# Starting the input projection after one eighth of the contraction, with its first sums parked in SBUF

## What is computed

```python
mod = jax.nn.silu(c) @ w_ada + b_ada                       # 2048 -> 6 * 2048, for 1 + 8 conditions
shift1, scale1, gate1, shift2, scale2, gate2 = [t[:, None, :] for t in jnp.split(mod, 6, axis=-1)]
h = rmsnorm(x, norm1_g) * (1 + scale1) + shift1
qa, ka, va, qb, kb, vb, r, log_a = project(h, w_in, ...)   # h @ w_in, 2048 -> 6160
oa = mix_a(qa, ka, va)                                     # dilated attention, biased by rel_bias
ob = mix_b(qb, kb, vb, log_a)                              # gated linear attention
x = x + gate1 * merge_out(oa, ob, r, a_out_g, gla_out_g, w_out, x.dtype)
h2 = rmsnorm(x, norm2_g) * (1 + scale2) + shift2
y, new_hist = conv_ffn(h2, conv_hist, w_up, conv_w, conv_b, w_down)
x = x + gate2 * y
```

## Time and profile before

| | us |
|---|---|
| median of 3 runs | 1544.39 |
| lowest, highest | 1542.82, 1545.78 |
| span of the profiled execution | 1544.0 |
| TensorE busy | 1514.8 (98%) |
| VectorE busy | 875.7 (57%) |
| ScalarE busy | 633.9 (41%) |
| first product of w_in starts | 44.23 |
| chunk 8 of w_in starts | 79.75 |

### The profile page before, as it was taken

One profiled execution on the slowest core, in us unless ns is written; L12 is line 12 of the kernel. 1 busy time (PEld: TensorE's weight loads), 2 busy tenths in 40 slices (PEclk: granted clock), 3 DMA queues, 4 the chain that ended last, 5 costly groups with the idle time before them and its releaser, 6 DMA issues.

```text
span 1544.0 us, 27862 instructions
## 1 busy us (share of the span) xinstructions
PE 1514.8 (98%) x11762; PEld 1372.8 (89%) x11762; DVE 875.7 (57%) x1509; ACT 633.9 (41%) x873; POOL 52.4 (3%) x89
## 2 busy tenths in 40 slices
PE   8999999999999889999999999999999999999999
PEld 4877888888888557768899999999999999999999
DVE  3655676666667435557454555555554565656574
ACT  3433444434445215235333333334333445545453
POOL 2000000001111000000000000000000000000000
PEclk8999999999999999999999999999999999999999
DMA  9998777777777997997644444454545444454541
GB/s 354 400 355 346 307 257 257 257 259 267 255 288 270 413 414 309 422 363 292 251 164 164 164 164 169 159 184 147 188 146 182 163 172 178 166 181 172 178 176 53
DMA packets 62283, 370.98 MB, mean 240 GB/s; under 512 B 7431, under 2 KB 7913, under 8 KB 27081
## 3 DMA queue, kind: packets, MB, share of 16 engines
q1 hardware_dynamic: 56096, 351.08, 60.6%
q0 software_dynamic: 5904, 17.93, 3.4%
q10 hardware_dynamic: 162, 0.22, 0.0%
HBM read 359.32 MB, written 9.88 MB: 239 GB/s over the span
## 4 chain that ended last, share of the span: by engine, by line
PE 89%; DMA 5%; DVE 3%; SPq 2%; ACT 1%; issue 1%; POOL 0%; ACTq 0%; DVEq 0%
PE ps L989 26%; PE ps L990 25%; PE ps L991 25%; PE ps L941 4%; PE ps L934 1%; SPq L710 1%; DMA ring<-in_w_ada_early 1%; DMA ring<-in_w_out 1%; DMA ring<-in_cache_k_win 1%; DMA proj<-in_tables 1%; ACT whi L1501 1%; DVE wlo L2028 1%; PE ps L1321 1%; DMA ring<-in_w_ada 1%; PE ps L1290 1%
## 5 line engine op out<-in xcount | busy, mean ns | idle before, releaser
L989 PE MATMUL ps<-hhi,whi 128*128 128x288 f32 x3136 | 934.0, 298 | 3.1 <-DVE wlo L1871 1.6
L990 PE MATMUL ps<-hlo,whi 128*128 128x288 f32 x3136 | 922.6, 294 | 0.0
L991 PE MATMUL ps<-hhi,wlo 128*128 128x288 f32 x3136 | 922.5, 294 | 0.0
L989 PEld LDWEIGHTS ps<-hhi,whi 128*128 128x128 f32 x3136 | 589.0, 188 | 38.8 <-issue 29.9
L990 PEld LDWEIGHTS ps<-hlo,whi 128*128 128x128 f32 x3136 | 589.2, 188 | 0.7
L991 PEld LDWEIGHTS ps<-hhi,wlo 128*128 128x128 f32 x3136 | 588.9, 188 | 0.0
L1492 ACT ACTIVATE whi<-ring 128x1024 fp32r<-128x1024 f32 x178 | 185.7, 1060 | 200.7 <-PE ps L991 200.7
L1864 DVE TENSOR_TENSOR wlo<-ring,whi 128x1024 fp32r<-128x1024 f32 x178 | 212.0, 1221 | 78.8 <-ACT whi L1492 78.4
L2028 DVE TENSOR_TENSOR wlo<-ring,whi 128x1024 fp32r<-128x1024 f32 x96 | 117.0, 1223 | 79.6 <-ACT whi L1501 79.5
L1501 ACT ACTIVATE whi<-ring 128x1024 fp32r<-128x1024 f32 x96 | 100.8, 1053 | 130.1 <-PE ps L991 114.2
L2545 DVE TENSOR_TENSOR wlo<-ring,whi 128x1024 fp32r<-128x1024 f32 (+1 forms) x94 | 105.7, 1132 | 56.2 <-ACT whi L1805 56.2
(11 more groups left out here) (298 smaller groups left out, 905.4 us busy)
## 6 DMA issues: line engine op xcount, KB each, us to landing
ring<-in_w_up SPq DMA_DIRECT2D x88, 1024.0 KB, 4.8
ring<-in_w_down SPq DMA_DIRECT2D x32, 1408.0 KB, 6.1
ring<-in_w_ada SPq DMA_DIRECT2D x42, 1024.0 KB, 6.8
ring<-in_w_in SPq DMA_DIRECT2D x28, 1024.0 KB, 6.5
ring<-in_w_ada_early SPq DMA_DIRECT2D x22, 1024.0 KB, 7.5
proj<-in_w_ada SPq DMA_DIRECT2D x22, 1024.0 KB, 11.0
ring<-in_w_in_early SPq DMA_DIRECT2D x20, 1024.0 KB, 9.3
ring<-in_w_out SPq DMA_DIRECT2D x16, 1024.0 KB, 13.2
```

Source lines behind the costliest of these rows:

```text
L989: mm(out, w_hi, x_hi, start=start, stop=False)
L990: mm(out, w_hi, x_lo, start=False, stop=False)
L991: return mm(out, w_lo, x_hi, start=False, stop=stop)
```

## The change

The eight slabs of group 0 are laid out anew: slabs 0 to 3 (half a) hold shift and scale of k-tiles 0 and 1, slabs 4 to 7 (half b) those of k-tiles 2 and 3. The first eight chunks become half chunks (`half_chunk`): each holds two k-tiles for four output tiles (a pair of units) in the banks 0, 1, 2 and 4, in the order of `HALVES`: four over k-tiles 0 and 1, four over k-tiles 2 and 3; the fourth and the fifth are of the same tiles and add up in PSUM. The sums of the first three and of the fifth are copied to `proj` (`half_copy`), those of the last three are added onto them. They have weights laid out for them, `w_in_first`. Slabs 4 to 7, the bias products and the second turn come between the half chunks; slab 0 goes ahead of the second half of x's transposes, slab 1 and the roots between them. Modulation is in two parts (`half_mod`, `half_norm`). The eight slabs of group 1 are used two behind each of chunks 4 to 7 and no longer two behind chunks 1, 3, 5 and 7. On ScalarE and VectorE the copies of emptied tiles stand ahead of the splitting of the next weights. On SP the first four w_in loads are asked for between the first w_ada slabs, and lead slabs earlier; some of the later w_ada slabs have new homes (`LEAD_HOMES`), and the counts for the ring's odd slots are shifted to suit. The bias tables are loaded to another place, once x is transposed.

```diff
--- before.py
+++ after.py
@@ -30,6 +30,9 @@
 NC9 = 1 + NB
+PAIR_TILES = (28, 32, 36, 24)
+HALVES = ((0, 0), (0, 1), (0, 2), (0, 3), (1, 3), (1, 0), (1, 1), (1, 2))
+LEAD_HOMES = "SSLLRRSSLLSSRRLLSSLLSSLL"
 DIL = ((128, 1), (512, 4), (2048, 16))
@@ -130,11 +133,17 @@
+    early = np.arange(2 * D).reshape(2, KD // 4, 2, 256)
+    early[:, 0] = early[:, 0].transpose(1, 0, 2).copy()
+    first = column_blocks(w_in[0, 0:D, 2048:5120], 4, 512)[:, 0].reshape(6, P, 4, 512)
+    first = np.stack([first[PAIR_TILES[q] // 4 - 4][:, 2 * z:2 * z + 2] for z, q in HALVES])
+    first = first.reshape(4, 2, P, 1024).transpose(0, 2, 1, 3).reshape(4, P, 2048)
     down = w_down[0].reshape(4, 11, P, D // 256, 256).transpose(3, 0, 2, 1, 4)
...
             "w_down": np.ascontiguousarray(down.reshape(D // 256, 4, P, 11 * 256)),
-            "w_ada_early": column_blocks(w_ada[0, :, 0:2 * D], 4, 512)}
+            "w_in_first": np.ascontiguousarray(first),
+            "w_ada_early": column_blocks(w_ada[0][:, early.reshape(-1)], 4, 512)}
...
@@ -490,6 +504,12 @@
+        def half_banks(r):
+            return (0, 1, 2, 4)[r]
+        def half_tile(j, r):
+            return PAIR_TILES[HALVES[j][1]] + r
         def bank_of(n, t):
@@ -524,27 +544,40 @@
-        ADA_AT = [s // 2 * 2 + 1 for s in range(22)] + [22, 22]
+        ADA_AT = [4 + s // 2 for s in range(8)] + [s // 2 * 2 + 1 for s in range(8, 22)] + [22, 22]
         LATE_AT = [23 + r // 2 * 4 for r in range(32)]
...
+            if s < 4:
+                return 0, (0, 2, 1, 3)[s], 16
             if s < 8:
-                return s // 4, (0, 2, 1, 3, 0, 1, 2, 3)[s], 16
-            a = s - 8
-            return (0, 1 + 2 * (a % 2), 32 + 16 * (a // 4)) if a % 4 < 2 else (2, a % 2, 16 + 16 * (a // 4))
+                return 1, (1, 3, 0, 2)[s - 4], 16
+            a, kind = s - 8, LEAD_HOMES[s - 8]
+            before = LEAD_HOMES[0:a].count(kind) // 2
+            if kind == "S":
+                return 0, 1 + 2 * (a % 2), 32 + 16 * before
+            if kind == "R":
+                return 1, (1, 3)[a % 2], 32 + 16 * before
+            return 2, a % 2, 16 + 16 * before
+        def lead_freed(a):
+            kind = LEAD_HOMES[a]
+            before = [b for b in range(a) if LEAD_HOMES[b] == kind and b % 2 == a % 2]
+            return 8 + before[-1] + 1 if before else a + 1
...
@@ -655,7 +690,7 @@
-                sp.wait_ge(raw_used, a + 5)
+                sp.wait_ge(raw_used, lead_freed(a))
                 ada_load(8 + a)
@@ -671,17 +706,26 @@
                 sp.dma_start(xr[0:NS, 2, cols], a["x_sample"].rearrange("b t d -> (b t) d")[:, cols]).then_inc(x_in[n], 16)
-            for s in range(8):
+            for s in range(3):
                 ada_load(s)
             in_load(0)
+            for s in range(3, 6):
+                ada_load(s)
             in_load(1)
-            for s in range(2):
-                sp.wait_ge(raw_used, s + 3)
-                ada_load(s + 8)
+            for s in range(6, 8):
+                ada_load(s)
+            sp.wait_ge(raw_used, 3)
+            ada_load(8)
+            in_load(2)
+            sp.wait_ge(raw_used, 4)
+            ada_load(9)
+            in_load(3)
             ada_load(10)
...
             ada_load(11)
+            lead_load(4)
+            lead_load(5)
             def unit_used(x):
@@ -713,8 +757,9 @@
-            asks = [(2 * w - 5.3, in_load, w) for w in range(2, 48)]
-            asks += [(ADA_AT[a_ - 4] + 1.2, lead_load, a_) for a_ in range(4, 24)]
+            asks = [(2 * w - 5.3, in_load, w) for w in range(4, 48)]
+            asks += [(ADA_AT[a_ - 6] + 0.5, lead_load, a_) for a_ in (6, 7)]
+            asks += [(ADA_AT[a_ - 4] + 1.2, lead_load, a_) for a_ in range(8, 24)]
             asks += [(LATE_AT[r - 2] + 1.4 if r >= 2 else ADA_AT[20 + r] + 1.2, late_load, r) for r in range(32)]
@@ -800,7 +845,8 @@
-            pool.wait_ge(full[1], 16)
+            pool.wait_ge(*PT_.upto("x15"))
+            pool.wait_ge(*NA[0].upto("q5"))
             c1 = CONST_LAYOUT["hot_s"][0]
...
@@ -951,6 +998,8 @@
                 i, half = s // 8, s // 4 % 2
+                if s == 8:
+                    pe.wait_ge(*PV_.upto("bias_s"))
                 if i and s % 4 == 0:
@@ -961,6 +1010,8 @@
                     pe.wait_ge(*AV.upto("mod", i - 1))
+                elif i == 0:
+                    pe.wait_ge(*PV_.upto("bias_p"))
                 ada_turn(6 if half else 5).then_inc(*AT.step("turn_b" if half else "turn_a"))
@@ -969,20 +1020,19 @@
             vectors()
+            early_slab(0)
             for k in range(8, KD):
                 x_turns(k)
-            for s in range(4):
-                early_slab(s)
-            norm_roots()
+                if k == 11:
+                    early_slab(1)
+                if k == 13:
+                    norm_roots()
+            early_slab(2)
+            idle_products(6, 2)
+            early_slab(3)
+            idle_products(6, 1)
+            early_turn(0, 0)
             idle_products(6, 4)
-            early_slab(4)
-            biases()
-            early_turn(0, 0)
-            for s in range(5, 8):
-                early_slab(s)
-            idle_products(3, 1)
-            early_turn(0, 1)
-            idle_products(7, 8)
@@ -1046,6 +1096,34 @@
                     between(c)
+            def half_chunk(j):
+                z = HALVES[j][0]
+                pe.wait_ge(lo_done, CH_IN + j + 1)
+                for r in range(4):
+                    if j in (1, 2, 3):
+                        pe.wait_ge(part_v if r % 2 else part_a, 2 * (j - 1) + r // 2 + 1)
+                    elif j > 4:
+                        pe.wait_ge(tile_v if r % 2 else tile_a, 2 * (j - 5) + r // 2 + 1)
+                    for k in range(2):
+                        if j in (0, 4):
+                            pe.wait_ge(*NL[0].upto(f"l{2 * z + k}", 0))
+                        w = slice(512 * k + P * r, 512 * k + P * r + P)
+                        last = three(ps[:, half_banks(r), 0:TOK], whi[:, j % BUFS, w], wlo[:, j % BUFS, w],
+                                     hhi[:, 2 * z + k, :], hlo[:, 2 * z + k, :], k == 0 and j != 4, k == 1 and j != 3)
+                    if r < 3:
+                        last.then_inc(tile_done, 1)
+                last.then_inc(used, 1)
+                if j == 0:
+                    early_slab(4)
+                if j == 1:
+                    early_slab(5)
+                    early_slab(6)
+                    biases()
+                    early_slab(7)
+                if j == 2:
+                    early_turn(0, 1)
@@ -1248,10 +1326,12 @@
-            pe.wait_ge(*PV_.upto("bias_s"))
-            pe.wait_ge(*NM[0].upto("ms"))
+            pe.wait_ge(*PV_.upto("x15"))
+            pe.wait_ge(*NM[0].upto("rs"))
             for j in range(LAST):
-                if j < CH_OUT:
+                if j < HALVED:
+                    half_chunk(j)
+                elif j < CH_OUT:
                     in_chunk(j)
...
@@ -1521,16 +1606,37 @@
             root(0, roots)
+            in_hi(0)
             ada_rows(0, 0)
+            norm_hi(0, (0, 1))
+            in_hi(1)
+            def half_copy(j, r):
+                act.wait_ge(tile_done, 3 * j + r + 1)
+                if j >= 2:
+                    act.wait_ge(*PV_.upto("bias_s"))
+                f(proj[:, half_tile(j, r), :], ps[:, half_banks(r), 0:TOK], ACT.Copy).then_inc(tile_a if j == 4 else part_a, 1)
+            half_copy(0, 0)
+            half_copy(0, 2)
+            in_hi(2)
+            in_hi(3)
+            half_copy(1, 0)
+            half_copy(1, 2)
             ada_rows(0, 1)
-            in_hi(0)
-            norm_hi(0)
-            for j in range(1, 4):
-                in_hi(j)
+            half_copy(2, 0)
+            in_hi(4)
+            half_copy(2, 2)
+            norm_hi(0, (2, 3))
+            in_hi(5)
+            half_copy(4, 0)
+            half_copy(4, 2)
+            in_hi(6)
+            in_hi(7)
...
                 act.wait_ge(used, CH_IN + BUFS + j + 1)
-                act.wait_ge(*PV_.upto("bias_s"))
+                act.wait_ge(tile_a, j)
                 f(proj[:, UNITS[CHUNKS[j][0]], :], ps[:, early_banks(j)[0], 0:TOK], ACT.Copy).then_inc(tile_a, 1)
@@ -1640,8 +1746,8 @@
-            for j in range(1, LAST):
-                if j <= FIRST:
+            for j in range(HALVED - 3, LAST):
+                if HALVED < j <= FIRST:
                     early_copy(j - 1)
...
@@ -1897,17 +2003,23 @@
-            def norm_roots():
+            def norm_sums():
...
                 v.tensor_scalar(roots, roots, 1 / D, EPS, ALU.mult, ALU.add).then_inc(*NM[0].step("ms"))
+            def norm_diagonals():
                 dve.wait_ge(*NA[0].upto("rs"))
...
                 last.then_inc(*NM[0].step("diag"))
+            def norm_roots():
                 dve.wait_ge(*NT[0].upto("roots"))
@@ -2020,9 +2132,42 @@
+            def half_mod(z):
```

(86 more changed lines are left out.)

49 lines of the change are left out of this document (31 added, 18 removed).

## The result

The changed kernel takes 1546.62 us in the median (1543.74 to 1549.6, 20 runs), the kernel before 1543.97 (1542.52 to 1545.78, 20 runs). The ratio is 1.0018, 95% interval 1.0012 to 1.0024: slower by 0.18%, just within the 0.2% that the prediction called no change. Predicted were 1540.0 and a range of 1537.7 to 1545.0, so the time lies above the range.

A forecast was written before the change was run, and what follows sets the result against it. TensorE alone was taken to set the pace from 44.2 us, so only the opening could win: first product 11.1 us earlier, less added work, 4.4 gained off the 1544.39 median, 1540.0 us; range 1537.7 to 1545.0.

The forecast's parts named there:

- I take the early side: Opening, TensorE's clock: full clock back by 24 us, since slabs come sooner; first product 32.6 to 33.9, taken as 33.1.
- The late end of the bounds: Opening: no clock rise before slab 3 has ended, first product at 38.7, gain -1.1 us.
- That copies go ahead of the next weights' parts costs nothing, as the weights' parts are three chunks ahead: ScalarE and VectorE queues during the half chunks: emptied tiles copied before the next weights are split, at zero cost.
- The prediction's list of landings: DMA arrivals of slabs and loads after the opening, at 2.55 us each; smallest margin at slabs 16, 17.
- The early clock: Opening at full clock by 24 us, all margins holding: 1540.0 us, chance 0.55, own range 1538.5 to 1541.3.
- no idle ahead of chunk 4 over 1 us: Sign that the forecast is right: TensorE waits no more than 1 us before chunk 4.
- What that start has to carry: TensorE from first product to chunk 8: 42.2 us with added slabs, biases and turn; chunk 8 at 75.3, 4.4 gained.
- at 2.55 us each: DMA transfers after the opening: 2.55 us for each MB, giving landings with uses 2 to 7 us later.
- The transfers become the bound: Rival, DMA: at 2.8 us per MB instead of 2.55 the gain shrinks to 0, 1544 us; chance 0.10.
- ScalarE waiting for w_in slabs: Sign of transfers as the bound, alongside TensorE waiting for slabs 5 to 7 or 14 to 17.
- the 27th slab: DMA: with slower transfers this slab would be 6.5 us late against a margin of 1.5 to 2.
- The shift travels to the end unchanged: After the opening: later stages are released by what products have used, so the opening's shift should reach the end.

The follow-up runs named there:

- slab_pair: Changed kernel with slab 1 directly behind slab 0, ahead of the second half of x's transposes; 1546.20 us, ratio 1.0020.
- warm: Changed kernel with four more idle products, two ahead of the condition's turns and two ahead of the small vectors; 1548.36 us, ratio 1.0031.
- kept_low8_less: kept_low8 without the three idle products on either side of slab 3; 1542.57 us, ratio 0.9987.
- after_third: Changed kernel, unedited, profiled a third time; 1544.35 us (one run).
- low8_behind: Changed kernel with VectorE's low part of chunk 8 moved behind chunk 5's adds; 1543.46 us, ratio 0.9998.
- kept_low8: Changed kernel with the edits of kept_clock and low8_behind together; 1541.54 us, ratio 0.9986.
- kept_clock: Changed kernel with nine idle products among x's first eight transposes and ahead of the small vectors, fourth w_ada slab asked before first w_in; 1546.45 us, ratio 1.0012.
- before_kept: Kernel before with nine idle products, behind each of x's first eight k-tiles and ahead of the small vectors; 1546.05 us, ratio 1.0017.
- again: Changed kernel once more, no edit, second profile; 1547.68 us, ratio 1.0021.

## Why the prediction was wrong

**"I take the early side" was the first step that failed.** The term is the clock's. With the rise by 24 us it gave a first product at 32.6 to 33.9; the three profiles have 38.49, 38.61 and 35.66, with the clock back at 33.8, 33.1 and 25.6. The late end of the bounds, 38.7, was right for two of three. The reason given, that slabs had raised the clock before and now come sooner, fell in slab_pair. The Trainium skill's page "TensorE: Matmul & The Clock Gate" (Part 4, PE-mode transpose) says that transposes don't engage the full clock, and read strictly it spoke for the late end; the traces side with it as far as x's second half goes, and warm adds that TensorE fell to 1.2 GHz while it did nothing but transposes. But eighteen transposes from 10.14 us ran at 2.4 GHz behind the idle products, and the changed kernel stayed at 1.2 GHz through slabs too, so the page alone would not have given 33.8 or 25.6.

**"That copies go ahead of the next weights' parts costs nothing, as the weights' parts are three chunks ahead" was the second, and it decides the sign.** I asked what a chunk loses if its own weights' part is late, and did not ask what stands behind that part in VectorE's queue. Being three chunks ahead is what hurts: the part of chunk 8 comes between chunk 4's copies and chunk 5's adds, and needs a load that lands at 65.1 to 67.0 us however early the opening is (69.1 in warm; asked for at 56.3 in kept_low8_less, landing at 66.0, and at 60.5 in after_third, landing at 67.0). The prediction's list of landings leaves this load out; between lead slab 5 (63) and 6 (68), by its 2.55 us each, there is room for it at some 65.5, an estimate; the profiles have 65.1 to 67.0. The early clock that I forecast would have met it: the first product at 33.1 puts chunk 6 at 63.6, and the landing at 66.7 plus 2.83 at 69.5, a wait of 5.9 us. That the order is the cause is shown by moving one line: low8_behind against the changed kernel (3.2 us of the median, each taken beside the kernel before: ratios 0.9998 and 1.0018), and kept_low8 against kept_clock in one session (4.9). No run moved the load instead, ahead of the w_ada slabs that are asked for before it; whether that would do as well is open. My check was "no idle ahead of chunk 4 over 1 us"; it held, and was two chunks too early.

**"What that start has to carry" held.** 42.2 us were predicted from first product to chunk 8, and 41.7 measured. Where neither the clock nor the queue is in the way, the sum works: kept_low8_less starts at 34.41 and its slabs behind chunk 7 are at 74.80 (78.31 in the changed kernel, which started 4.08 later: 3.51 kept). The first product itself was set too early even for a full clock, 33.1 against 34.41 to 35.99. Keeping the clock has a price: the nine idle products take some 0.5 us each, and slab 0 starts at 20.09 (kept_low8) and 20.80 (kept_low8_less), against 16.41 in the changed kernel. A cheaper way wasn't tried.

**Transfers.** The steady estimate "at 2.55 us each" put no late slab in TensorE's way, and none was. The rival "The transfers become the bound" named as its sign "ScalarE waiting for w_in slabs", and that is there in each profile of the changed kernel and its variants, 1.60 to 6.59 us; but its mechanism, the 27th slab, was another, and what makes ScalarE's wait cost time is VectorE's order.

**The shift travels to the end unchanged**: to 509 us it does, in every kernel within 0.1 us (2.87 at 316 us and 2.83 at 509 in kept_low8). From 509 to 700 each execution adds 189 to 194 us, whatever it brought along.

**How the median comes about.** The mean of the marks at 316 us is 317.35 in the changed kernel's three profiles and 315.86 in the two of before: 1.5 of the 2.65 us. Wait and low clock behind it cost 0, 4.96 and 0.75 us in the three, 1.9 in the mean, where moving the line took 3.2 off the median. The rest is open, and so is before_kept's 2.4 us. Its opening is as before; in a second execution it didn't move by more than 0.3 us; the stretch from 509 to 700 us was the longer one in its profiles (192.0 and 193.2, against 192.1 and 189.1), but two each are no proof that idle products in the first 20 us lengthen a stretch 500 us later.

## What to carry to other kernels

Where a queue prepares operands several steps ahead, each such step stands in front of work that frees the next bank; write down for each what it waits for, and put the emptying of a bank ahead of a part whose load may be late. An earlier start is only worth what the first shared resource behind it can follow: here a load that landed no sooner than 65.1 us whatever the opening did, so that a start 2.8 us earlier became a mark at 316 us that is 2.1 us later (again against the first profile). And where a clock has two levels, weigh both in the forecast, not the one that the last profile happened to show, since the same program came back to 2.4 GHz at 25.6 and at 33.8 us.
